# Two-block transformer forward on one core: the first feed-forward works on h times the norm's gain, and the pool layer's norm sums its squares on VectorE

## The reference, cut to what matters

```python
h = h + rms_norm(mix, post_mix_norm)                        # norm 1
f = conv_ffn(rms_norm(h, pre_ffn_norm), w_up, conv_w, conv_b, w_down)   # norm 2 ahead of w_up
h = h + rms_norm(f, post_ffn_norm)                          # norm 3
e = rms_norm(p @ w_ple, ple_norm)                           # norm 4
h = h + sigmoid(h @ w_ple_gate) * e
y = h * rsqrt(mean(h * h) + eps) * (1 + scale) * g + shift  # norm 5, ahead of the pool layer's w_in

def conv_ffn(x, w_up, conv_w, conv_b, w_down):
    hu = x @ w_up                       # 1024 -> 5632: 22 gate tiles and 22 up tiles of 128
    hu = causal_depthwise_conv3(hu, conv_w) + conv_b
    gate, up = split(hu, 2)
    return (gelu(gate) * up) @ w_down
```

## Time and profile before

| What | Before |
|---|---|
| Median of three runs | 1380.52 us (1375.64 to 1382.44) |
| The profiled execution | 1378.35 us, its span 1376.6 us |
| TensorE matmuls busy | 1304.8 us, 95% of the span |
| VectorE / ScalarE / GpSimd busy | 40% / 46% / 61% |
| Granted TensorE clock, mean | 0.966 of full |
| First feed-forward, tile 0 to the end of the down product | about 353.5 to 544.6 us |
| Norm 3 to the last gate tile | 544.6 to 574.5 us |
| Norm 5 to the pool layer's first matmul | 574.5 to 586.7 us |

### The profile page before, as it was taken

One profiled execution on the slowest core, in us unless ns is written; L12 is line 12 of the kernel. 1 busy time (PEld: TensorE's weight loads), 2 busy tenths in 40 slices (PEclk: granted clock), 3 DMA queues, 4 the chain that ended last, 5 costly groups with the idle time before them and its releaser, 6 DMA issues.

```text
span 1376.6 us, 26036 instructions
## 1 busy us (share of the span) xinstructions
PE 1304.8 (95%) x10869; PEld 1219.9 (89%) x10869; DVE 546.4 (40%) x1230; ACT 628.0 (46%) x971; POOL 840.4 (61%) x426
## 2 busy tenths in 40 slices
PE   6997989879999999998999999999999999999998
PEld 5983548669999999898999999999998888999997
DVE  5658686633455562323433204022222224433302
ACT  5530443135555553554544434464634554544431
POOL 7984400026488787555788776755645655888781
PEclk9997989989899999899999999999999999999998
DMA  8759985503355555325455554453537783455550
GB/s 263 196 177 344 350 320 187 184 1 123 125 183 184 176 191 184 123 92 184 154 184 184 168 177 146 154 154 91 179 118 246 241 283 103 157 182 184 169 166 31
DMA packets 232819, 242.83 MB, mean 176 GB/s; under 512 B 9069, under 2 KB 201727, under 8 KB 232703
## 3 DMA queue, kind: packets, MB, share of 16 engines
q1 hardware_dynamic: 232382, 241.08, 53.8%
q10 hardware_dynamic: 320, 0.10, 0.0%
HBM read 240.11 MB, written 1.05 MB: 175 GB/s over the span
## 4 chain that ended last, share of the span: by engine, by line
PE 75%; DVE 1%; ACT 1%; issue 1%; ACTq 0%; DVEq 0%
PE banks L548 75%; DVE banks L1629 0%; DVE hn L1629 0%; ACT hn_hi L2356 0%; DVE h L1622 0%; PE banks L558 0%; DVE h L1629 0%; ACT arena L2356 0%; ACT ring_hi L2356 0%; ACT hn L2356 0%; ACT rs L2356 0%; ACT L2356 0%; DVE rs L1635 0%; ACT banks L2356 0%; ACT eT_hi L2356 0%
## 5 line engine op out<-in xcount | busy, mean ns | idle before, releaser
L1562 POOL TENSOR_TENSOR ring_lo<-ring,ring_hi 128x2048 fp32r<-128x2048 f32 (+1 forms) x176 | 719.0, 4096 | 463.7 <-ACT ring_hi L2356 463.3
L548 PE MATMUL banks<-hn_hi,ring_lo 128*128 128x256 f32 (+1 forms) x1864 | 527.2, 287 | 0.0
L548 PE MATMUL banks<-hn_hi,ring_hi 128*128 128x256 f32 x1696 | 481.5, 288 | 9.5 <-ACT hn_hi L2356 9.0
L548 PE MATMUL banks<-hn_lo,ring_hi 128*128 128x256 f32 x1696 | 444.2, 283 | 0.0
L2356 ACT ACTIVATE ring_hi<-ring 128x2048 fp32r<-128x2048 f32 (+1 forms) x176 | 299.4, 1704 | 173.2 <-PE banks L548 134.5
L548 PEld LDWEIGHTS banks<-hn_hi,ring_lo 128*128 128x128 f32 (+1 forms) x1864 | 365.0, 196 | 0.1
L548 PEld LDWEIGHTS banks<-hn_hi,ring_hi 128*128 128x128 f32 x1696 | 332.3, 196 | 11.4 <-issue 9.6
L548 PEld LDWEIGHTS banks<-hn_lo,ring_hi 128*128 128x128 f32 x1696 | 309.9, 192 | 0.1
L2356 ACT ACTIVATE arena<-banks 128x256 f32<-128x256 f32 (+6 forms) x231 | 90.4, 409 | 258.5 <-PE banks L548 203.1
L548 PEld LDWEIGHTS banks<-arena 64*128 64x128 f32 (+4 forms) x1282 | 117.2, 181 | 68.3 <-issue 48.2
L548 PE MATMUL banks<-arena 128*64 128x128 f32 (+9 forms) x1282 | 144.9, 307 | 27.0 <-issue 12.7
(11 more groups left out here) (257 smaller groups left out, 1612.4 us busy)
## 6 DMA issues: line engine op xcount, KB each, us to landing
ring<-in_ada_w_dram SPq DMA_DIRECT2D x48, 1024.0 KB, 7.8
ring<-in_ffn_w_up_dram SPq DMA_DIRECT2D x44, 1024.0 KB, 5.2
ring<-in_w_up_dram SPq DMA_DIRECT2D x22, 1024.0 KB, 5.2
ring<-in_ffn_w_down_dram SPq DMA_DIRECT2D x16, 1024.0 KB, 5.2
ring<-in_w_kv_dram SPq DMA_DIRECT2D x15, 1024.0 KB, 5.5
ring<-in_w_in_dram SPq DMA_DIRECT2D x9, 1024.0 KB, 8.7
ring<-in_w_kv_dram SPq DMA_DIRECT2D x18, 512.0 KB, 4.1
ring<-in_attn_w_q_dram SPq DMA_DIRECT2D x18, 512.0 KB, 3.9
```

Source lines behind the costliest of these rows:

```text
L548: return nc.tensor.matmul(o, l, r, start=start, stop=stop, **k)
L1562: led.emit(g.tensor_tensor(low, raw, high.bitcast(F32), ALU.subtract), sem("lo_ready"))
```

## The change

Five things, besides renumbered counts.

1. `add_normed` goes; norm 1 uses `add_normed_split` with a gain: the high parts of `h` times `pre_ffn` are made as `h` itself is, and the tiles of `w_up` are computed on them, without norm 2's root.
2. Norm 2's squares are taken by ScalarE tile by tile in the same loop, and its sums go between the matmuls of `first_tiles`, which now has 3 tiles and not 4. Norm 1's four banks (`spread_kept`) are held through this. `spread(2, False)`, `ada_columns()`, `ple(6)` and `ple(7)` come after `first_tiles`.
3. Each of the 44 up tiles is multiplied on VectorE by the root's reciprocal (`wide_sb`, a copy in SBUF) in its bank before ScalarE's `own` reads it.
4. `second_gains` goes behind the first pair of the feed-forward, and GpSimd's small block behind its sixteenth `low_parts`.
5. Norm 5 joins `SUMMED`: `projection(2, "pg", ..., (5, sqb))` holds a bank for its sum from the start, ScalarE squares each tile of `h` as it is ready, VectorE adds them, and the table for the root is loaded after the last square and not before the first.

```diff
         dint = at(12288, 2, T)
+        wide_sb = at(12800, T)
...
-        SUMMED = (1, 3, 6, 7, 8, 9)
+        SUMMED = (1, 3, 5, 6, 7, 8, 9)
...
             square_base[i] = square_count
-            square_count += 8 if i in SUMMED else 0 if i == 4 or i == 0 else 5
+            square_count += 8 if i in SUMMED or i == 2 else 0 if i == 4 or i == 0 else 5
...
                 if i in (1, 3):
-                    return (sem("h_ready"), KT) if i == 1 else (sem("x_split"), KT * 4)
+                    return sem("x_split"), KT * (3 if i == 1 else 4)
...
                     return sem("x_split"), KT * (8 if job == ("xs", 7, 0) else 9)
-                return sem("x_split"), KT * {0: 1, 2: 3, 5: 5, 6: 7, 8: 11}[i]
+                if i != 2:
+                    return sem("x_split"), KT * {0: 1, 5: 5, 6: 7, 8: 11}[i]
...
-            def first_tiles(rnd, jobs, x, ks=tuple(range(KT)), ms=None):
+            def first_tiles(rnd, jobs, x, ks=tuple(range(KT)), ms=None, norm=None):
                 low, high = x
                 todo = []
+                if norm is not None:
+                    b_ms = opened(("ms", norm[0]))
                 if ms is not None:
                     gathered(ms)
                 for job, key, c0 in jobs:
@@ -610,6 +614,8 @@
                     for b, (w_lo, w_hi) in todo:
                         mm(b, w_hi[:, k, :], high[:, k, :], start=(n == 0), stop=False)
...
                         mm(b, w_lo[:, k, :], high[:, k, :], start=False, stop=False)
+                    if norm is not None:
...
                     if i in SUMMED and k == 0:
                         copied(("acc", i))
-                    elif i in SUMMED:
...
                         last = mm(b[p * HD:p * HD + HD, s * P:s * P + P],
                                   gn_small[:, 1, c, s, p:p + 1].broadcast_to([P, HD]), ident[:, :])
                 close(last)
+            def spread_kept(i):
+
+                kept = [held_back() for _ in range(4)]
+                for x in range(3):
+                    numbered(("xs", i, x), kept[x])
+                numbered(("wd", i), kept[3])
+                pe.wait_ge(sem("rs_small"), NORM_ORDER.index(i) + 1)
+                for s in range(2):
+                    last = mm(banks[:, kept[3], s * P:s * P + P], rs_of(i)[:, 2 + s:3 + s].broadcast_to([P, P]), ident[:, :])
+                close(last, 4)
...
+                return kept
+
             projection(0, "out", "out", (hn_lo, hn_hi), (1, sqb), (3, 4, 5, 6, 7, 0, 1, 2))
             ple(2)
-            spread(1)
+            kept = spread_kept(1)
             down_used = [0]
             def ffn(f, first, ms):
                 tiles = [((nm, f, 2 * i + x), (nm, f, i), 128 * x) for i in range(FT // 2) for nm in ("ug", "uu")
                          for x in range(2)]
-                first_tiles(first, tiles[:4], (hn_lo, hn_hi))
-                for t in tiles[4:]:
+                begin = 4 if f else 3
+                first_tiles(first, tiles[:begin], (hn_lo, hn_hi), norm=None if f else (2, sqb))
+                if f == 0:
+                    for bank in kept:
+                        held.remove(bank)
+                    spread(2, False)
+                    ada_columns()
+                    ple(6)
+                    ple(7)
+                for t in tiles[begin:]:
                     split_tile(*t, (hn_lo, hn_hi))
...
                 mean_square_of(ms[0], b_ms, ms[1], (0, 6, 7))
                 spread(ms[0], f < 2)
-            ada_columns()
             for m in (3, 4, 5):
                 ple(m)
-            mean_square(2, hn)
...
-            ple(7)
-            spread(2)
             ffn(0, 1, (3, sqb))
-            projection(2, "pg", "pleg", (hn_lo, hn_hi))
-
-
-            mean_square(5, hn)
-            spread(5)
+            projection(2, "pg", "pleg", (hn_lo, hn_hi), (5, sqb))
             def grouped(gq):
                 for i in range(2):
...
                              sem("x_split"))
             order = sorted(split_no, key=split_no.get)
-            low_parts(order[:10])
+            low_parts(order[:16])
             pool.wait_ge(sem("gains"), 4)
             led.emit(g.iota(dint.bitcast(mybir.dt.int32), pattern=[[P, 2], [-1, T]], base=0, channel_multiplier=1))
             led.emit(g.tensor_copy(bdist[:, 0, :, :], dist[:, :, :]))
             keep_if(bdist[:, 0, :, :], ALU.is_ge, P, -1, [[-P, 2], [1, T]], FAR, sem("late_consts"))
             first_out = split_no["do", 0]
-            low_parts(order[10:first_out])
+            low_parts(order[16:first_out])
             attention_low(range(5))
             low_parts(order[first_out:first_out + 1])
...
@@ -2137,8 +2137,12 @@
                         own_done(scaled[k - 1])
                         tt(x[(k - 1) % 3], h[:, k - 1, :], x[(k - 1) % 3], ADD, sem("h_ready"))
                     if k >= 2:
-                        dve.wait_ge(sem("h_copied"), k - 1)
-                        tt(low[:, k - 2, :], x[(k - 2) % 3], high[:, k - 2, :].bitcast(F32), SUB, sem("x_split"))
+                        dve.wait_ge(sem("h_copied"), KT * (rnd - 1) + k - 1)
+                        if next_gain is None:
+                            tt(low[:, k - 2, :], x[(k - 2) % 3], high[:, k - 2, :].bitcast(F32), SUB, sem("x_split"))
+                        else:
+                            stt(low[:, k - 2, :], x[(k - 2) % 3], col(next_gain, k - 2), high[:, k - 2, :].bitcast(F32),
+                                MUL, SUB, sem("x_split"))
             def ffn(f):
                 W0, B0, n = (row0["conv_w"], row0["conv_b"], 44) if f == 0 else \
...
+                        tt(b[:, 0:T], b[:, 0:T], wide_sb, MUL, sem("normed"))
+                        if between is not None:
+                            act_low(between)
                     dve.wait_ge(sem("conv_own"), conv_base[f] + (4 * (j // 2) + 2 * x + j % 2 if f == 0 else j) + 1)
                     t = ct[:, j % 2, x, :]
                     w = W0 + 22 * x + j
                     stt(t[:, 1:T], b[:, 0:T - 1], par[:, w + n:w + n + 1], t[:, 1:T], MUL, ADD)
                     first_tap = led.count["dve_own"]
-                    if between is not None:
+                    if f and between is not None:
                         act_low(between)
                     dve.wait_ge(sem("dve_own"), first_tap)
                     stt(t[:, 2:T], b[:, 0:T - 2], par[:, w:w + 1], t[:, 2:T], MUL, ADD,
                         *((sem("conv_done"),) if f == 0 and x == 0 else freed((nm, f, j))))
+                if f == 0:
+                    dve.wait_ge(*freed(("wd", 2)))
                 for j in range(0, FT, 2):
                     convolved(0, j, j - 1 if j else None)
...
+                    if f == j == 0:
+                        modulation_before(("uu", 0, 2))
+                        settle()
...
                 add_square(1, k, sqb)
-            add_normed(1, "post_mix", yb)
-            scaled_parts(2, lambda k: col("pre_ffn", k), 1, hn_hi, hn_lo, sem("x_scaled"))
-
-            for n, (l, sc, gn) in enumerate(((0, 1, cols("norm1", 8)), (0, 4, cols("norm2", 8)), (2, 1, cols("kv_norm", 8)),
-                                             (1, 1, cols("norm1", 8, 8)))):
-                c0 = 48 * l + 8 * sc
-                stt(gsc[:, 8 * n:8 * n + 8], mod[:, c0:c0 + 8], 1.0, gn, ADD, MUL, sem("gains"))
+            add_normed_split(1, "post_mix", yb, 1, hn_hi, hn_lo, "pre_ffn")
+            placed(("ms", 2))
+            rec(rs_of(2)[:, 2:4], rs_of(2)[:, 0:2], sem("rs_small"))
+
+            def second_gains():
+
+                for n, (l, sc, gn) in enumerate(((0, 1, cols("norm1", 8)), (0, 4, cols("norm2", 8)), (2, 1, cols("kv_norm", 8)),
+                                                 (1, 1, cols("norm1", 8, 8)))):
+                    c0 = 48 * l + 8 * sc
+                    stt(gsc[:, 8 * n:8 * n + 8], mod[:, c0:c0 + 8], 1.0, gn, ADD, MUL, sem("gains"))
+
             ffn(0)
             dve.wait_ge(sem("eb_squares"), 4)
...
@@ -2245,6 +2263,8 @@
                     g, n = gated[m - 1]
                     own_done(n)
                     stt(h[:, m - 1, :], g, 0.5, h[:, m - 1, :], MUL, ADD, sem("h_ready"))
+                if m >= 4:
+                    add_square(5, m - 3, sqb)
...
-                    b = take((("ug", "uu")[x], f, j))
+                    if f == 0:
+                        reach((("ug", "uu")[x], f, j))
+                        act_.wait_ge(sem("normed"), 4 * (j // 2) + 2 * x + j % 2 + 1)
+                        b = bank_of((("ug", "uu")[x], f, j))
+                    else:
+                        b = take(("ug", f, j))
                     if j >= 2:
                         act_.wait_ge(sem("act_ready" if x or f else "gate_act"), FT * f + j - 1)
...
-            squares(hn, h_at(0), (3, 4, 5))
+            x = norm_slots(1)
+            for k in range(KT):
+                if k < 3:
+                    ple(3 + k)
+                act_.wait_ge(sem("h_ready"), k + 1)
```

(21 more changed lines are left out.)

41 lines of the change are left out of this document (10 added, 31 removed).

## The result

The changed kernel takes 1398.74 us (median of 4 runs, 1390.49 to 1404.18) against 1381.48 for the kernel before beside it: a ratio of 1.0116, 95% interval 1.0087 to 1.0146. It is slower, as forecast, but by 17 us and not by 8, and it lies outside the range (1380 to 1394). The profiled execution is the slowest of the four, 1404.18; its span is 1402.4.

The account below looks back on a forecast made before the run. TensorE was taken to bound the kernel, its matmuls covering 95% of the span. Terms 4.9 + 8.0 - 5.1 gave 7.8 us slower, 1388.3 us on the median of 1380.5; range 1380 to 1394.

Parts of the forecast that it names:

- first bank wait: First feed-forward: fifth tile ug2 waits for ug0's bank, released by act_low(0), 358.1 to 367.0; with part 1, 4.9 us slower.
- Part 3: Gate tiles after norm 3: pg3 waits for xs0's bank until all low parts are made; 8.0 us slower, at most 1 back.
- Part 4: Norm 5, last gate tile to first pool matmul: fewer sum instructions on TensorE and the root starts earlier; 5.1 us faster.
- rivals A and B: Both bank waits absent (A, 12.1 us faster, 5%), or only one there (B, 1380.3 or 1376.4 us, 10%).
- rival A: Banks come back in time, so part 1 and Part 4 stand alone: 12.1 us faster, 1368.4; chance 5%.
- Rival D: Gate tiles: square on ScalarE needs another table than tanh, two loads per tile from the third; about 13 us more, 1401; 3%.
- part 1: TensorE up to the fourth tile: merged loop at 1.2 us per k, eight times; four tiles end 7 us earlier.
- Rival C: Clock falls inside the merged loop, which takes 17 us instead of 9.6; 7.4 us more, 1395.7; chance 7%.
- A third was kept in the bounds only: First feed-forward, tile ug3 behind the bank wait: it may also run at half clock, up to +2.2 us.

Follow-up runs that it names:

- c0: The changed kernel run once more, unaltered, as the standard of the follow-up group; median 1391.94 us, ratio 1.0087 to the kernel before.
- e2: Changed kernel with the gate projection begun with three tiles side by side instead of four; median 1386.13 us, ratio 1.0044 to the kernel before.
- e9: Kernel before with only the change's norm 5 part added; median 1386.55 us, ratio 1.0036 to the kernel before.
- e10: Kernel before with only the norm 5 part, and three first gate tiles instead of four; median 1376.98 us, ratio 0.997 to the kernel before.
- e1: Changed kernel with the four banks that are free first numbered for tiles ug2, ug3, uu2, uu3; median 1380.57 us, ratio 0.9997 to the kernel before.
- e12: e7 with five extra ScalarE activations so TensorE idles some 3.5 us ahead of the merged loop; median 1379.75 us, ratio 0.9973 to the kernel before.
- e14: e12 with 28 unread 256-column matmuls ahead of the wait, filling the idle time; median 1372.85 us, ratio 0.9932 to the kernel before.
- e7: Changed kernel with e1's and e2's edits together and the gain products moved behind the third pair of tiles; 1370.2 us, ratio 0.9928 to the kernel before.
- e11: Changed kernel with gain products' first operand from PSUM, in tile 1's half bank (output wrong, timing only); median 1390.78 us, ratio 1.0063 to kernel before.
- e17: Changed kernel with gain products' first operand from PSUM, in the half bank of uu 1; median 1391.17 us, ratio 1.0074 to the kernel before.
- e16: e7 with ScalarE reading the three ple products in a row ahead of its conversion loop; median 1370.69 us, ratio 0.9917 to the kernel before.
- e8: e7 with 14 extra unread 256-column matmuls right ahead of the merged loop; median 1373.82 us, ratio 0.9938 to the kernel before.

## Why the prediction was wrong where it was wrong

**Right.** The first bank wait is there with its releaser. From norm 1's sums to ug2 it was to be 34.3 us (367.0 - 332.74); c0, the loop at full clock, has 33.98 (368.20 - 334.22). Part 3 was to be 8.0 and is 8.0; e2 got back 5.8 to 7.4 in time, and e9 with e10 9.6. Part 4 was to be 5.1 and the table's line has 5.0, but part of that agreement is luck: from the last gate tile's end to the pool's first matmul it is 7.6 us and not 7.1, so 4.6 were gained there, since the 12 sum instructions ran at half clock and took 2.4 us; the other 0.4 lies in the gate tiles, 24.8 us and not 25.2, which is the give-back that part 3 had in its bounds. e10 shows 4.1 in the median alone. The count of banks, which rivals A and B denied, held at both places, and e1 measured what rival A would have given for the first: 11.4 against 12. Rival D did not come: no table load stands in the gate tiles. On the table itself the rows decide against the drain of 1.38 us that the Trainium skill adds ("ScalarE: Activation LUTs", section "What ACT_TABLE_LOAD costs"): in the changed kernel's timeline of ScalarE the load follows the last square by 0.14 us and the next activation follows the load at once, as in the earlier trace rows.

```profile
604.34 0.42 ACT L2376 ACTIVATE arena<-h 128x256 f32<-128x256 f32 x1 [0.25 <-DVE h L1643]
...
604.90 1.28 ACT L2376 ACT_TABLE_LOAD   x1
606.19 0.20 ACT L2376 ACTIVATE drv<-drv 128x1 f32<-128x1 f32 x1
```

**The step that failed** is part 1's "6 matmuls (0.72) and 4 sum instructions (0.48), 1.2 us, eight times": it priced the loop at full clock in every execution. In the profiled execution it took 16.1 us and the low pass behind it 3.9 and not 2.9, 7.5 us over. Rival C had this with its size (7.4) and its place, at 7%, set low because "the idling here is 1 us". The idling was 1.5 to 1.6, and e12 against e14 shows that this was the right thing to look at and the wrong conclusion: by their times, 3.5 us bring the fall in nine of twelve runs and no idle time in none of six. With 1.5 to 1.6 us both were profiled: the loop fell in the changed kernel's first profile and in e1's, and held 2.4 GHz in c0's, e2's, e7's, e11's and e17's. The forecast should have been two numbers some 8 us apart.

**A second term was missing**: the gain products, 4.3 us beside GpSimd's product. The prediction moved `second_gains` and costed it at nothing, without asking what GpSimd does at the new place. ug3 started 7.6 us behind ug2 and not 5.8, in both profiles, 1.8 more. The wait ahead of it was 2.1 us in c0 and 2.7 in the first profile, and 0.85 in e17, where the products are short; so they cost 1.3 to 1.9 us there, and in c0 the rest is ug2, which ran all its 24 matmuls at half clock and not 20. **A third was kept in the bounds only, and is there in one profile only**: in the first, ug3 ran its first 15 matmuls at half clock too, 1.4 us (15 x 0.093); in c0's it ran at full clock. With the second term, and the loop at full clock, the forecast is 1381.9 (before, beside c0) + 4.9 + 1.8 + 8.0 - 5.0 = 1391.6; c0 has 1391.94. With 1.4 for ug3 and 7.5 for the loop it is 1400.5, near the three highest of the two sets (1401.27, 1403.22, 1404.18).

**Still open.** What makes 1.5 us of idle time enough in one execution and not in the next isn't shown, nor how much of it is the idle time and how much the one-column sums and the short spread ahead of it: no run has the wait without them. The Trainium skill ("TensorE: Matmul & The Clock Gate", section "Part 1: The HAM clock gate") says that the points at which the chip judges activity run on by themselves and don't start with the kernel; that would give such a spread, and no run here shows it. Nor is it shown whether the loop of e16 is safe from it: six runs and one profile say so, at 0.9 us of idle time.

## What to carry to other kernels

Count the banks in opening order whenever a change removes scratch jobs or holds a bank: here two waits of 8.6 and 10 us, which a list of four banks and one tile fewer took away, made a change that is worth 11 us look like a loss of 10. When work of few columns goes into a loop that follows even a short idle time of TensorE, price the loop at both clocks, and look for the wait ahead of it, since that is the cheap thing to mend. A small VectorE instruction with two inputs in SBUF is only small if GpSimd is idle at its place. And when executions vary as these do, compare profiles over the stretch that the change touches, and medians only beside the kernel before on the same chip.

## What the runs showed of the hardware

The same instructions, in the same order, ran at 2.4 GHz in one execution (c0, 1.62 us of idle time ahead) and at 1.2 GHz for all but the first microsecond of a 16 us loop in another (1.54 us of idle time ahead, the loop 3 us later from the span's start). TensorE was never idle in that loop. Matmuls whose result nobody reads can pay: e14 issues 28 of them and is some 5.5 us faster than e12. They pay only for the idle time that e12 had added; against e7 they bring nothing (0.9932 and 0.9928 of the kernel before).

VectorE's four instructions of 128x8 with both inputs in SBUF ended 0.25 to 0.26 us behind the end of GpSimd's 128x2048 product in each of the changed kernel's, c0's, e1's, e7's and e8's profiles, after 4.2 to 4.4 us for four, of which the longest one took 4.0 to 4.2; with only one input in SBUF, eight of the same size took 0.75 us while that product ran (e17). The Trainium skill has the rule ("SBUF — State Buffer", section "SBUF: two separate sides"): a VectorE instruction with two inputs in SBUF and a GpSimd one that reads SBUF shut each other out for a whole instruction. The changed kernel's trace agrees, with 4.1 us for one that takes 0.15.
